# Two weight places in place of three for the experts, and a gather of y rows in two passes

## What is computed

```python
def hier_moe(h, w_rg, b_rg, w_re, b_re, w_e_in, w_e_out):
    g_prob = jax.nn.softmax((x @ w_rg) + b_rg); g_top, g_idx = lax.top_k(g_prob, 1)
    e_logits = ((x @ w_re) + b_re).reshape(NT, N_GROUPS, EXPERTS_PER_GROUP)
    ...
    def expert_block(args):
        xs, e = args                                   # xs: a block of tokens, 1024 wide
        gate, up = jnp.split(xs @ w_e_in[e], 2, axis=-1)      # w_e_in[e]: 1024 x 1024
        return (jax.nn.silu(gate) * up) @ w_e_out[e]          # w_e_out[e]: 512 x 1024
    yb = lax.map(expert_block, (xb, block_exp)).reshape(n_slots, D)
    y = jnp.zeros((NT, D), f32).at[slot_tok].add(yb.astype(f32) * slot_w[:, None])

x = x + gt2 * hier_moe(h, ...)
```

## Time and profile before

| what | value |
|---|---|
| time, median of 3 (lowest, highest) | 1766.65 us (1766.56, 1767.51) |
| profiled execution: time / span | 1765.35 / 1763.6 us |
| TensorE (PE) busy | 1646.5 us, 93% |
| VectorE (DVE), ScalarE (ACT), GpSimd (POOL) busy | 1110.1, 537.9, 372.6 us |
| granted TensorE clock, mean | 0.975 |
| expert stage (first product of expert 0 to end of the last) | 1204.0 to 1719.9 us |
| from there to the end of the span | 43.7 us |
| DMA traffic | 386.77 MB, of it q1 304.72 MB |

### The profile page before, as it was taken

The page is one execution under the profiler, slowest core; times in us unless marked ns, Lnnn a source line. Parts: engine busy times, 40 slices in busy tenths (PEclk is TensorE's granted clock), DMA queues, the critical chain, the costliest instruction groups (busy, mean ns, idle before and its releaser), DMA issues.

```text
span 1763.6 us, 36677 instructions
## 1 busy us (share of the span) xinstructions
PE 1646.5 (93%) x15177; PEld 980.8 (56%) x15177; DVE 1110.1 (63%) x2641; ACT 537.9 (31%) x1235; POOL 372.6 (21%) x471
## 2 busy tenths in 40 slices
PE   5999999999999899999999999986999999999990
PEld 3455444454444677777677645554566566665560
DVE  2486616655776455666665635564887878887754
ACT  5221323433443223333323321113333333332310
POOL 3030000000223564455664350110000000000003
PEclk9999999999999999999999999997999999999995
DMA  9377219100222422142122187568999999999998
GB/s 350 124 247 274 72 51 324 35 25 24 84 84 96 145 63 58 43 141 67 43 64 60 63 270 276 203 238 347 405 423 424 423 423 423 425 423 423 425 378 307
DMA packets 137720, 386.77 MB, mean 219 GB/s; under 512 B 13914, under 2 KB 83464, under 8 KB 124300
## 3 DMA queue, kind: packets, MB, share of 16 engines
q1 hardware_dynamic: 113744, 304.72, 45.5%
q10 hardware_dynamic: 15708, 50.54, 7.6%
q0 software_dynamic: 8112, 29.23, 4.5%
HBM read 331.10 MB, written 66.08 MB: 225 GB/s over the span
## 4 chain that ended last, share of the span: by engine, by line
PE 76%; DMA 9%; DVE 8%; SPq 3%; issue 2%; ACT 1%; POOL 1%; ACTq 0%; POOLq 0%; DVEq 0%
PE bank L342 75%; DMA arena<-in_w_e_in 5%; SPq L466 2%; DVE arena L2645 1%; DMA arena<-in_w_ada 1%; DVE arena L2635 1%; DMA arena<-y_slots,ints 1%; PE bank L1092 1%; DMA arena<-in_w_in 1%; DVE arena L2373 0%; POOL arena L906 0%; PE bank L1412 0%; DVE arena L2076 0%; DMA arena<-token_blocks 0%; DVE arena L2324 0%
## 5 line engine op out<-in xcount | busy, mean ns | idle before, releaser
L342 PE MATMUL bank<-arena 128*32 128x256 f32 (+11 forms) x14798 | 1603.6, 381 | 43.6 <-issue 4.1
L342 PEld LDWEIGHTS bank<-arena 128*32 128x32 f32 (+4 forms) x14798 | 934.9, 133 | 686.4 <-issue 433.7
L1917 ACT ACTIVATE arena<-arena 128x96 f32<-128x96 f32 (+1 forms) x372 | 151.8, 497 | 219.9 <-DVE arena L2635 219.9
L2635 DVE STREAM_TRANSPOSE arena<-arena 32x192 f32<-32x192 f32 x496 | 183.6, 370 | 6.5 <-ACT arena L1908 0.2
L2645 DVE STREAM_TRANSPOSE arena<-arena 32x128 f32<-32x128 f32 x384 | 158.4, 412 | 4.8
L906 POOL DMA_INDIRECT arena<-y_slots,ints x16 | 16.4, 1023 | 537.0 <-DMA y_slots<-arena 531.1
L826 POOL TENSOR_TENSOR arena<-arena 64x256 f32<-64x256 f32 x96 | 70.2, 731 | 59.3 <-DVE arena L2343 52.5
L2618 DVE TENSOR_TENSOR arena<-arena,bank 128x128 f32<-128x128 f32 x96 | 21.9, 283 | 92.8 <-ACT arena L1926 92.3
L2367 DVE TENSOR_TENSOR arena<-arena,bank 128x128 f32<-128x128 f32 (+1 forms) x40 | 11.3, 283 | 74.2 <-PE bank L342 74.2
L1926 ACT ACTIVATE arena<-bank 128x128 f32<-128x128 f32 x96 | 19.6, 276 | 111.2 <-PE bank L342 111.2
L2076 DVE RECIPROCAL arena<-arena 128x512 f32<-128x512 f32 x10 | 33.5, 3349 | 30.1 <-ACT arena L1620 30.1
(11 more groups left out here) (356 smaller groups left out, 1335.5 us busy)
## 6 DMA issues: line engine op xcount, KB each, us to landing
arena<-in_w_e_in SPq DMA_DIRECT2D x64, 2048.0 KB, 26.2
arena<-in_w_e_out SPq DMA_DIRECT2D x32, 2048.0 KB, 28.2
arena<-in_w_ada SPq DMA_DIRECT2D x12, 2048.0 KB, 12.8
arena<-in_w_in SPq DMA_DIRECT2D x48, 512.0 KB, 4.3
arena<-x_slots ACTq DMA_DIRECT2D x31, 384.0 KB, 11.1
y_slots<-arena ACTq DMA_DIRECT2D x32, 288.0 KB, 14.6
y_slots<-arena POOLq DMA_DIRECT2D x21, 384.0 KB, 18.2
arena<-in_w_in SPq DMA_DIRECT2D x3, 2048.0 KB, 21.7
```

What stands on the lines that cost most here:

```text
L342: return nc.tensor.matmul(o, l, r, start=start, stop=stop)
L1917: ins = A.activation(e_xT[s][:, k, QT * w:QT * (w + n)].rearrange("p (w m) -> p w m", m=QT), raw_columns(c, k % 2, w, n), ACT.Identity, sc ...
L2635: ins = V.transpose(e_raw[ts(b, QT), :, ts(g, QT)], pieces[:, :, b, :])
```

## The change

- The third place is used once, for expert 2, under the name `WX` and one semaphore (`merge_w`). From expert 3 on the experts alternate between `WE[0]` (odd e) and `WE[1]` (even e).
- TensorE no longer has experts 4 to 31 written out: steps 4 to 31 and closes 3 to 30 are a loop of 14 turns over two experts. SP's loop is over two experts as well.
- All 8 tiles have a place for their y rows: six in the third place's columns (24576 to 36864), two in `WE[1][0]`. `f_x` moves into `WE[1][1]` and `WE[1][2]`.
- The gather has two passes. The first reads rows of experts 0 to 28 (`EARLY` = 29; numbers beyond are skipped by the bounds check) when y of expert 28 is stored; tiles 6 and 7 also wait for expert 30's output product. The second, at the place of the old gather, uses `i_l1`, `i_l2`, where numbers of experts 0 to 28 are moved out of bounds, so it writes only what is missing.
- VectorE makes `i_l1` and `i_l2` in `blocks_placed` with four small instructions. SP loads x1 after expert 30's output product and after the first gathers of tiles 4 and 5. Tiles 0 and 1, 2 and 3, 4 and 5 share a semaphore, and VectorE waits for the gathers of both tiles of such a pair.

```diff
-        WE.append([view(32768, 4, 1024), view(24576, 4, 1024), view(28672, 4, 1024)])
+        WX = [view(32768, 4, 1024), view(24576, 4, 1024), view(28672, 4, 1024)]
-        f_x = [view(24576 + 1024 * t, D) for t in range(NT)]
-        f_y = [[view(2048 * i, D), view(2048 * i + 1024, D)] for i in range(4)]
+        EARLY = NE - 3
+        FY = (0, 0, 1, 1, 2, 2, 3, 4)
+        f_x = [view(16384 + 1024 * t, D) for t in range(NT)]
+        f_y = [[view((24576 if t < 6 else 0) + 2048 * t + 1024 * k, D) for k in range(TOPK)] for t in range(NT)]
...
             next_in(3, 0, 1)
             next_in(4, 1, 2)
             next_out(3, 0, 1)
-            next_in(5, 2, 3)
             next_out(4, 1, 2)
-            with sp.Fori(2, (NE - 2) // 3) as i:
...
+            next_in(5, 0, 4)
+            with sp.Fori(3, NE // 2) as i:
+                next_in(2 * i, 1, 2 * i - 1)
+                next_out(2 * i - 1, 0, 2 * i - 2)
+                next_in(2 * i + 1, 0, 2 * i)
+                next_out(2 * i, 1, 2 * i - 1)
+            next_out(NE - 1, 0, NE - 2)
-            sp.wait_ge(sem("y"), 2 * (NE - 2))
+            sp.wait_ge(sem("y"), 2 * (NE - 1))
+            sp.wait_ge(fy_in[2][0], fy_in[2][1] + 64)
             for t in range(NT):
                 sp.dma_start(f_x[t], x1_t[t]).then_inc(sem("gate_in"), 16)
...
+            pool.wait_ge(sem("y_st0"), 32 * ((EARLY + 1) // 2))
+            pool.wait_ge(sem("y_st1"), 32 * (EARLY // 2))
+            for t in range(NT):
+                if t == 6:
+                    pool.wait_ge(sem("y"), 2 * (NE - 1))
+                for k, ix in enumerate((i_s1, i_s2)):
+                    pool.indirect_dma_start(out=f_y[t][k], out_offset=None, in_=yslot_d[0:EARLY * CAP],
+                                            in_offset=bass.IndirectOffsetOnAxis(ap=ix[:, t:t + 1], axis=0),
+                                            bounds_check=EARLY * CAP - 1, oob_is_err=False)\
+                        .then_inc(fy_in[FY[t]][0], 16)
...
             for t in range(NT):
-                if t >= 4:
-                    pool.wait_ge(sem("f_sum"), t - 3)
-                for k, ix in enumerate((i_s1, i_s2)):
-                    pool.indirect_dma_start(out=f_y[t % 4][k], out_offset=None, in_=yslot_d,
...
+                if t % 2 == 0 or t == NT - 1:
+                    pool.wait_ge(fy_in[FY[t]][0], fy_in[FY[t]][1] + 32 * FY.count(FY[t]))
+                for k, ix in enumerate((i_l1, i_l2)):
+                    pool.indirect_dma_start(out=f_y[t][k], out_offset=None, in_=yslot_d,
+                                            in_offset=bass.IndirectOffsetOnAxis(ap=ix[:, t:t + 1], axis=0),
+                                            bounds_check=NB * CAP - 1, oob_is_err=False)\
...
-            for e in range(3, NE):
-                step(e, e % 2, e % 3, e // 3)
-                close(e - 1, (e - 1) % 3, (e - 1) // 3)
...
+            with pe.Fori(2, NE // 2) as i:
+                e = 2 * i
+                step(e, 0, 1, i - 1)
+                close(e - 1, 0, i - 1)
+                step(e + 1, 1, 0, i)
+                close(e, 1, i - 1)
+            close(NE - 1, 0, NE // 2 - 1, e_hTl)
...
+                link(TS(r_over, r_div, float(EARLY * CAP), float(8 * T), ALU.is_lt, ALU.mult))
+                link(TT(r_over, r_over, r_div, ALU.add))
+                for a, isl in enumerate((i_l1, i_l2)):
+                    V.tensor_copy(isl, r_over[:, :, a])
...
-                y0, y1 = f_y[t % 4]
-                dve.wait_ge(fy_in[t % 4][0], fy_in[t % 4][1] + 32 * (t // 4) + 32)
+                y0, y1 = f_y[t]
+                dve.wait_ge(fy_in[FY[t]][0], fy_in[FY[t]][1] + 64 * FY.count(FY[t]))
```

More of the change, by code:

```diff
@@ L588, in _ @@
                 sp.wait_ge(sem(f"x_sc{t}"), 16 * NT)
-            w_out_of(2, 2)
+            sp.dma_start(WX[2], I["w_e_out"][0, 2:3].rearrange("a (p k) n -> p (a k) n", p=P)).then_inc(sem("merge_w"), 16)
             def next_in(e, s, used):
@@ L626, in _ @@
             with sp.If(n_extra > 0):
+                sp.wait_ge(sem("router_dve"), X_TABLE)
                 with sp.Fori(0, NX) as j:
@@ L1492, in step @@
             def step(e, s, w, turn):
-                pe.wait_ge(sem(f"win{w}0_in"), 16 * turn + 16 + begun(f"win{w}0_in"))
+                pe.wait_ge(sem(f"win{w}0_in"), 16 * turn + 16)
                 pe.wait_ge(sem("e_xT"), e + 1)
@@ L1496, in step @@
                 first(s, WE[w], 0).then_inc(sem("win_half"), 1)
-                pe.wait_ge(sem(f"win{w}1_in"), 16 * turn + 16 + begun(f"win{w}1_in"))
+                pe.wait_ge(sem(f"win{w}1_in"), 16 * turn + 16)
                 first(s, WE[w], 1).then_inc(sem("win_used"), 1)
@@ L1501, in close @@
                 pe.wait_ge(sem("e_hT"), e + 1)
-                pe.wait_ge(sem(f"wout{w}_in"), 16 * turn + 16 + begun(f"wout{w}_in"))
+                pe.wait_ge(sem(f"wout{w}_in"), 16 * turn + 16)
                 pe.wait_ge(sem("y_out"), 2 * e)
@@ L1518, in _ @@
             second(WE[0])
-            step(2, 0, 2, 0)
-            close(1, 1, 0)
-            for e in range(3, NE):
-                step(e, e % 2, e % 3, e // 3)
-                close(e - 1, (e - 1) % 3, (e - 1) // 3)
-            close(NE - 1, (NE - 1) % 3, (NE - 1) // 3, e_hTl)
+            pe.wait_ge(sem("merge_w"), 80)
+            pe.wait_ge(sem("e_xT"), 3)
+            pe.wait_ge(sem("e_act"), 2)
+            first(0, WX, 0).then_inc(sem("win_half"), 1)
+            first(0, WX, 1).then_inc(sem("win_used"), 1)
+            close(1, 1, 0)
+            step(3, 1, 0, 1)
+            pe.wait_ge(sem("e_hT"), 3)
+            pe.wait_ge(sem("y_out"), 4)
+            second(WX)
+            with pe.Fori(2, NE // 2) as i:
[5 more added lines that the diff above has]
+            close(NE - 1, 0, NE // 2 - 1, e_hTl)
             pe.wait_ge(sem("router_dve"), EXTRAS)
```

33 lines of the change are left out of this document (11 added, 22 removed).

## The result

The changed kernel took 1786.76 us (median of 4 runs, 1783.47 to 1789.07) against 1766.61 us of the kernel before beside it: ratio 1.0116, interval [1.0095, 1.0137]. The forecast was 1783 us in a range of 1773 to 1803. The profiled execution took 1786.52 us with a span of 1784.8 us, 21.2 us longer than the span in the earlier trace rows. The total is near the forecast by luck: the parts are off by more than the sum, and their errors cancelled.

A forecast was written before the change was run, and what follows sets the result against it. The weight transfers on q1 were taken as the bound. Last product 1719.9 + 14 (two places) + 0 (loop) + 3 (early gathers) = 1737, plus tail 43 = 1780 of span, plus 3 = 1783 us; range 1773 to 1803.

The forecast's parts named there:

- What bounds the kernel: Expert stage after 1204 us: weight queue q1 bounds it, 16.9 us an expert against TensorE's 15.55; lost q1 time returns almost whole.
- rival (c): Expert stage: q1 makes up the 13 us deficit before expert 25, only the shorter tail counts, 1761 us; chance 0.07.
- the +14 taken: Two weight places for three: q1 short of queued loads by 1274 us, last product 14 us later (bounds +11 and +16).
- Part 2: TensorE's loop of 14 turns: 13 backward turns at 2 us each, hidden while TensorE waits for transfers, so +0.
- Rival (b): TensorE's loop: the turn is the bound, 1800 us at 4 us a turn; chance 0.26 with 2.1 to 4 us.
- The cover of 2.1 us a turn: TensorE's loop: 27 us of slack before expert 31, thought to hide turns up to 2.1 us each.
- Part 3: First gather pass beside q1's last three loads: its bytes delay the last product by 3 us.
- Rival (a): End of the expert stage: gathers and x1 fit between the weights without collision, 1775 us; chance 0.17.
- Part 4: Tail after the last product: second gather pass, VectorE's sixteen steps and late x1 take 43 us (bounds 38 and 47), before 43.7.
- my +5: Tail: x1's rows load behind the gathers, there 19 us after the last product and not 13.8, adding 5 us.
- Rival (d): Second gather pass: skipped rows are fetched anyway, so it costs a pass over all rows, 1789 us; chance 0.05.
- The hole: q1 between 1241 and 1274 us: too few loads queued with two places, 4.90 MB or 13.2 us behind.

The follow-up runs named there:

- e3: Changed kernel with TensorE's experts written out and one pass of gathers, so only the two weight places remain: 1783.4 us, ratio 1.0094 to the kernel before.
- e1: Changed kernel without the first gather pass; one pass fetches all rows, two places and TensorE's loop stay: 1773.2 us, ratio 1.0033 to the kernel before.
- e9: Kernel before with experts 6 to 29 on TensorE in a loop of six experts a turn: 1797.3 us, ratio 1.0178.
- e12: Changed kernel with one pass of gathers and TensorE's loop over four experts a turn in place of two: 1807.8 us (one run).
- e2: Changed kernel with TensorE's loop written out, two places and both gather passes kept: 1782.7 us, ratio 1.0091 to the kernel before.
- e11: Changed kernel with eight gathers free to run early, the other eight held until expert 31's input product is done: 1777.2 us (one run).
- e4: Changed kernel with the first gather pass held until expert 31's input product is done: 1776.6 us, ratio 1.0053 to the kernel before.
- e6: Changed kernel with all but the first four early gathers held until expert 31's input product is done: 1772.3 us (one run).

## Why the prediction was right in sum and wrong in its terms

- **What bounds the kernel, and rival (c).** Right. q1's lost time came back at the end; with everything else undone (e3) two places cost 15.5 us by the medians, at the upper edge of the bounds of +11 to +16, and 17.6 in the last product, outside them, against the +14 taken. In the changed kernel q1 was 5.75 MB behind at 1300 us, which is 15.4 us, where the working had 15. Also right: 20.97 MB by 1274 us, expert 5's issue, and the first waits near expert 20.
- **Part 2, the loop, +0.** The sign was right for TensorE's own time and the term was wrong: -10 in e1, about -8 in the changed kernel (14 forecast, 5.8 arrived). The reading that failed took the instruction row only as the possible price of a turn. That row was traffic of the written-out code, on DMA engines that the same reading had just found full, and a loop that is held removes it; by the bytes this is 4.5 to 5.3 of the 8 to 10 us, and the rest is open. The range for a turn was bounded below at nothing "since a turn can cost nothing"; no row excluded a gain, and I should have kept one.
- **Rival (b), the turn as the bound.** Wrong for this body, right in kind: at four experts a turn the stop is there, 4.9 us where I had estimated 4. The rule quoted from the Trainium skill (Runtime: NRT & Kernel Launch, Instruction fetch mechanics) disagrees with this trace at two experts a turn, where a body of some 73 KB, more than two of its 16 KiB blocks, turned 13 times without a stop or a transfer; it agrees with e9 and e12. The same section of the Trainium skill also gives TensorE 128 KiB of instruction memory where most engines have 32. That size lies between the body that was held and the ones that were not; the prediction passed over it. The cover of 2.1 us a turn that I set against it hid nothing in e9 and e12, whose stops came back whole. That a stop of 5 to 10 us outlasts what the places let q1 run ahead would explain it; many small stops were not tried.
- **Part 3, the gather ahead, +3.** The step that went most wrong. The gathers were costed as bytes beside q1's bytes. The share was right: from 1705 to 1715 us, while both had work, q0 moved 0.84 MB and q1 2.88, 23% for a fifth. But these bytes cost nothing that e2 against e3 could show. The true cost, 14.0 us in the product and up to 1.8 after it, is on TensorE's issue, for which no row of the trace before could stand: there, TensorE was written out and the gathers came after it. Rival (a), no collision, named the right question for the bytes and missed this. An experiment with either edit alone would have shown nothing.
- **Part 4, the tail, 43.** Right in sum (43.3), by another path. x1, my +5, was not late itself. The second pass starts 10.9 us after the last product and not 5.8. The profile puts this wait down to the gather of tile 7 (14.70 us before 1752.41), but at this place the program asks of that semaphore only a count reached long before; it does wait for expert 31's y rows. The last part of their store was issued at 1742.46 and q10 moved bytes of it until 1751, beside x1 and the gathers of tiles 6 and 7, while before it was issued at 1720.82 and the first gather ran at 1725.73. So x1 may have cost its 5 us by delaying this store; no run separates it from the gathers. VectorE then started 6.7 us after the first gather where 8 was taken, and its sixteen steps had two gaps of 1.1 us where none was. Rival (d) is right in one respect: a gather whose rows are mostly skipped costs GpSimd its full 1.00 + 0.30 us, and q0 counts 2304 packets more for the same bytes. By those bytes the skipped rows weren't fetched; yet the page's figure for HBM reads rose by one pass's 8.39 MB (331.10 to 339.49), which I can't explain.
- **The sum.** The hole and the loop together +5.8 for +14, the product beside the gathers and what followed it +15.8 for +3, the tail -0.4 for -0.7: 8.2 too much, 13.1 too little, so 4.8 us of span and 3.8 us of the median.

## What to carry to other kernels

Where the DMA engines are full, the code of a long written-out engine program is part of the traffic: read the instruction queue's row, and consider a loop whose body is small enough to be held, then look at a run for stops at its turns. Look, too, at what runs beside the loop: here GpSimd's gathers slowed a looped TensorE, and the code right behind the loop, in some places and not in others, and even four could do it, so place them outside the loop and check the matmuls per 3 us. Cost a pair of edits for what they do to each other, and when a forecast comes out right, check its terms against the trace all the same.

## What was not expected of the hardware

- A loop of TensorE with a body of about 73 KB (an estimate, as are the next two sizes) ran 14 turns without a stop or a code transfer; 147 KB stopped 4.9 to 5.8 us a turn, 221 KB 9.0 to 10.2 us.
- With a held loop in place of 0.90 MB of code transfers q1 moved 1.98 MB more in the same 400 us (e3 to e1), and 1.69 MB more between e2 and the changed kernel.
- Gathers on GpSimd can slow a looped TensorE from 56 to between 8 and 16 matmuls in 3 us, ending 1 to 2 us after the last gather, and the written-out product right behind the loop to 21 (e11); in e4 and e6 they did not. The granted clock fell to the 1.2 GHz level some 5 us into it in the changed kernel; in e11 it stayed at 1.00 beside 8 us of slow issue.
- In the stretch of 1705 to 1720 us q0 moved 2.77 MB and q1 3.01 MB, but q1's loads ran out near 1715: 1.92 MB of q0's came after that. An even split of such a stretch says nothing of how the two queues share.
